# Letting GpSimd subtract the rounded weights in the SSD stage of a two-block network kernel

## The reference

```
u = rmsnorm(h); z, xbc, dt_raw, q, k, v, g_ssd, g_att = split_cols(u @ w_in)
xbc = silu(causal_dwconv(xbc, conv_w, conv_b));  xs, bm, cm = split_cols(xbc)
dt = softplus(dt_raw + dt_bias);  a = -exp(a_log)
for each chunk of 128 tokens (the first has 16), for each of 4 groups of 8 heads:
    L = exp(cs_l - cs_s) below the diagonal, cs = cumsum(dt * a)
    y = ((C B^T) * L) (x dt)  +  exp(cs) * C state
    state = exp(cs_last) * state + B^T (decay * x dt)
y = y + d_skip * x;  y = group_rmsnorm(y * silu(z)) ;  y_ssd = y @ w_ssd_branch
```

## Time and profile before

| what | value |
|---|---|
| median of 3 runs | 2701.64 us (2695.93 to 2713.91) |
| the profiled execution | 2691.95 us |
| its span, first to last instruction | 2690.0 us |
| TensorE busy | 2522.0 us (94%) |
| VectorE busy | 1632.3 us (61%) |
| ScalarE busy | 899.1 us (33%) |
| GpSimd busy | 62.2 us (2%) |
| mean granted TensorE clock | 0.965 of full |
| SSD stage's loop | about 1386 to 1862 us of the span |

### The profile page before, as it was taken

The page is one execution under the profiler, slowest core; times in us unless marked ns, Lnnn a source line. Parts: engine busy times, 40 slices in busy tenths (PEclk is TensorE's granted clock), DMA queues, the critical chain, the costliest instruction groups (busy, mean ns, idle before and its releaser), DMA issues.

```text
span 2690.0 us, 40344 instructions
## 1 busy us (share of the span) xinstructions
PE 2522.0 (94%) x15581; PEld 2210.7 (82%) x15581; DVE 1632.3 (61%) x2776; ACT 899.1 (33%) x1341; POOL 62.2 (2%) x55
## 2 busy tenths in 40 slices
PE   6999999998988999999989899889998999999997
PEld 4887888876887987888888788879777789999997
DVE  6556444456387845444587687877554555884684
ACT  3122222234354532222336634652232233222222
POOL 0000000000021000000000000001000000000000
PEclk9999999999988999999999999989998999999998
DMA  4235222334441012222225223412111112223222
GB/s 139 94 102 124 94 94 94 135 118 121 137 114 41 24 63 83 94 94 94 94 80 126 80 71 108 112 58 90 45 54 50 56 63 95 78 88 117 93 94 95
DMA packets 89708, 242.46 MB, mean 90 GB/s; under 512 B 24870, under 2 KB 56102, under 8 KB 65574
## 3 DMA queue, kind: packets, MB, share of 16 engines
q1 hardware_dynamic: 29056, 198.26, 20.7%
q10 hardware_dynamic: 58744, 36.42, 6.2%
q0 software_dynamic: 1760, 5.77, 1.0%
HBM read 230.50 MB, written 11.14 MB: 90 GB/s over the span
## 4 chain that ended last, share of the span: by engine, by line
PE 48%; DVE 8%; issue 3%; ACT 2%; ACTq 0%; DVEq 0%
PE ps L1151 26%; PE ps L927 13%; PE ps L1239 3%; DVE wlo L1389 1%; PE ps L1327 1%; PE ps L1294 1%; ACT L L776 1%; PE ps L1329 1%; PE ps L1330 1%; PE ps L1310 1%; PE ps L1313 0%; PE ps L1293 0%; ACT whi L506 0%; PE ps L1202 0%; PE ps L1204 0%
## 5 line engine op out<-in xcount | busy, mean ns | idle before, releaser
L506 ACT ACTIVATE whi<-raw 128x2048 fp32r<-128x2048 f32 x187 | 357.6, 1912 | 754.3 <-PE ps L927 501.5
L1151 PE MATMUL ps<-parts,whi 128*128 128x264 f32 x2752 | 488.6, 295 | 5.3 <-issue 4.7
L1389 DVE TENSOR_TENSOR wlo<-raw,whi 128x2048 fp32r<-128x2048 f32 x187 | 427.4, 2286 | 66.6 <-ACT whi L506 65.8
L927 PE MATMUL ps<-parts,whi 128*128 128x512 f32 x1360 | 435.0, 401 | 14.7 <-DVE wlo L1389 9.9
L1151 PEld LDWEIGHTS ps<-parts,whi 128*128 128x128 f32 x2752 | 396.2, 193 | 19.4 <-issue 16.7
L927 PEld LDWEIGHTS ps<-parts,whi 128*128 128x128 f32 x1360 | 259.0, 191 | 80.0 <-DVE wlo L1389 9.3
L927 PE MATMUL ps<-parts,wlo 128*128 128x512 f32 x680 | 271.8, 400 | 0.0
L1151 PE MATMUL ps<-parts,wlo 128*128 128x264 f32 x1200 | 247.4, 288 | 0.0
L927 PE MATMUL ps<-Mhi,whi 128*128 128x512 f32 x512 | 203.2, 397 | 5.1 <-DVE Mlo L1480 5.1
L927 PE MATMUL ps<-Mhi,wlo 128*128 128x512 f32 x512 | 203.0, 396 | 0.0
L927 PE MATMUL ps<-Mlo,whi 128*128 128x512 f32 x512 | 203.0, 396 | 0.0
(11 more groups left out here) (355 smaller groups left out, 4050.4 us busy)
## 6 DMA issues: line engine op xcount, KB each, us to landing
raw<-in_stream SPq DMA_DIRECT2D x187, 1024.0 KB, 4.8
csb<-sums_d ACTq DMA_DIRECT2D x16, 512.0 KB, 5.6
bands<-scratch ACTq DMA_DIRECT2D x6, 1024.0 KB
near<-bands ACTq DMA_DIRECT2D x20, 256.0 KB, 2.6
csf<-sums_d ACTq DMA_DIRECT2D x32, 128.0 KB, 6.0
Qst<-parts POOLq DMA_DIRECT2D x14, 256.0 KB, 6.3
tabs<-bands ACTq DMA_DIRECT2D x8, 418.0 KB, 3.0
X<-in_x SPq DMA_DIRECT2D x4, 512.0 KB, 14.8
```

The lines of the kernel that those rows point to most:

```text
L506: nc.scalar.activation(whi[:, s, :], raw[:, s, :], ACT.Copy).then_inc(hi_done, 1)
L927: mm = nc.tensor.matmul(out, w[:, s, at], x(k), start=k + j == 0, stop=k == k_tiles - 1 and j == 2)
L1151: mm = nc.tensor.matmul(ps[:, 2 * par + h, 0:HALF], w[:, s, at], x[:, k, h * HALF:(h + 1) * HALF], start=k + j == 0, stop=k == k_tiles - 1 ...
L1389: nc.vector.tensor_tensor(wlo[:, s, :], raw[:, s, :], whi[:, s, :].bitcast(F32), ALU.subtract).then_inc(lo_done, 1)
```

## The change

In the SSD stage, VectorE's 28 calls of `split_low` are taken out. GpSimd does the subtraction in four instructions of 512 columns a unit, two at a step: parts 0 and 1 at the even steps from 2 on, parts 2 and 3 at the odd ones, each time behind the Hd multiply of that step if there is one. The last two parts of the last unit come after the step loop. `lo_done` rises with the fourth part. VectorE gets one wait of its own for `lo_done` before its next subtract, in "kv2".

```diff
+            def split_low(c, turn, part):
+
+                u = U0["half"] + c + 2
+                s, at = u % 2, slice(part * SEQ, (part + 1) * SEQ)
+                if part == 0:
+                    pool.wait_ge(hi_done, turn + (u + 1))
+                    pool.wait_ge(lo_done, turn + u)
+                low = nc.gpsimd.tensor_tensor(wlo[:, s, at], raw[:, s, at], whi[:, s, at].bitcast(F32), ALU.subtract)
+                if part == 3:
+                    low.then_inc(lo_done, 1)
...
                         nc.gpsimd.tensor_tensor(Hd[:, :].rearrange("p (h d) -> p h d", h=SSD_HPG), Hs[:, :].rearrange("p (h d) -> p h d", h=SSD_HPG),
                                                 decay, ALU.mult).then_inc(hd_ready, 1)
+                    if r > 1:
+                        for part in (0, 1) if r % 2 == 0 else (2, 3):
+                            split_low(r // 2 - 1, i * 14, part)
+                for part in (2, 3):
+                    split_low(13, i * 14, part)
...
-                    if r and r % 2 == 0:
-                        split_low("half", r // 2 - 1, i * 14)
...
-                    if r % 2:
-                        split_low("half", r // 2, i * 14)
...
+            dve.wait_ge(lo_done, U0["kv2"] + 2)
             split_low("kv2", 0)
```

## The result

The kernel after takes 2711.01 us (median of 20 runs, 2705.62 to 2723.67); the kernel before took 2700.99 us beside it (20 runs, 2686.43 to 2713.91). The ratio is 1.0051, with an interval of 1.0034 to 1.0067: half a per cent slower, well inside 1%. The forecast was 2696, the likeliest case a small gain. The time lies inside the range of 8 in 10 (2683 to 2713), but on the other side of no change, nearer to rival one (2717).

The account below looks back on a forecast made before the run. TensorE, busy 94%, sets the time; in the SSD stage it waits for VectorE. Terms sum to -2.1 us a pass, twice -4.2, with (h) -1.8: -6.0, median 2696 us; range of 8 in 10: 2683 to 2713.

Parts of the forecast that it names:

- rival one: SSD stage: GpSimd/VectorE lock and late parts compound, clock falls at steps 10 and 16; slower, 2717 us; chance 0.2.
- (a): Steps 9 to 11: removed subtracts save at most 2.8 us a pass; with collisions, -0.8 taken.
- (d): Step 15: decay multiply comes sooner, at most 2.2 of a 4.40 us wait; -1.5 us a pass taken.
- (f): Step 17: subtract ahead of the multiply goes, 2.2 of 2.94 us plus slow stretch; -3.0 us a pass.
- (g): Step 20: subtracts ahead of YNlo and the last Gv add go; -3.3 us a pass after 0.7 collision.
- (h): Once, at the stage's end: subtract ahead of the output scale goes; -1.8 us of a 2.20 us wait.
- (b): Step 8: last parts, queued behind Hd, finish after TensorE's half tile would start; +0.7 us a pass.
- (c): Step 10: last parts, queued behind Hd, finish after TensorE's half tile would start; +2.8 us a pass.
- (e): Step 16: last parts behind Hd come late for TensorE; 2.4 us, with some collision +3.0 a pass.
- the shared resource: GpSimd and VectorE hold each other up; each part can stop a VectorE instruction wanting two SBUF inputs up to 1.25 us.
- point of decision: Sign deciding for rival one: a part holds VectorE for more than 1 us in most scan steps.
- I cost it at nothing: SP's stream load waits for the same semaphore; with at least 10 us spare before ScalarE rounds, its delay costs nothing.

Follow-up runs that it names:

- small_dve: Kernel before, with VectorE's subtract in the stage cut to 4 columns (that work left out): 2666.65 us, ratio 0.9870.
- small_pool: Kernel after, with GpSimd's parts cut to 4 columns at the same queue places (that work left out): 2678.56 us, ratio 0.9912.
- early: Kernel after, with all four parts of a unit at the even step, none at odd steps: 2706.7 us, ratio 1.0021.
- extra_pool: Kernel before, VectorE's subtracts kept, plus 112 GpSimd subtracts of 128x512 on their own tiles that nobody waits for: 2726.74 us, ratio 1.0083.
- whole: Kernel after, with one GpSimd instruction of 2048 columns per unit at the even step instead of four parts: 2739.19 us, ratio 1.0146.
- c12_dve: Kernel after, with one unit of each pass (c = 12, awaited by the pass's last load) subtracted by VectorE again: 2701.19 us, ratio 1.0003.
- branch_only: Kernel before, with only units 10 to 13 (branch sums) moved to GpSimd, four parts at the even step: 2705.02 us, ratio 1.0017.
- second_only: Kernel before, with only units 6 to 9 (second group's scans and norm) moved to GpSimd, four parts at the even step: 2684.18 us, ratio 0.9950.

## Why the prediction was wrong

The mechanism was seen and its size was not. The kernels make a chain from before to after, in us of the whole stage; beside each link stands what the sum had for it:

| link | measured | in the sum |
|---|---|---|
| before to small_dve: VectorE's subtract goes | -30.8 | -26.2: (a) 2.8, (d) 2.2, (f) 3.0 and (g) 4.0 twice, (h) 2.2 |
| small_dve to small_pool: GpSimd's instructions in their places, tiny | +5.6 | nothing |
| small_pool to early: full length, TensorE no longer waiting for them | +29.0, of which 2.2 at the pass boundary | +8.4 (hold), nothing (boundary) |
| early to after: the last parts a step later, behind Hd | +11.0 | +11.8: (b) 0.7, (c) 2.8 and (e) 2.4 twice |
| before to after | +14.8 | -6.0 |

(small_pool has a slow stretch of its own at the boundary; against before the boundary costs 4.2 us in early.) The hold in the sum is 2.0 us in (a), 0.7 in (d), 0.6 in (e) and 0.7 in (g), twice, and 0.4 in (h). Each link is a difference of two single profiled executions. The ratios, over all runs, check them: as us of 2701 they give the stage's difference from before to within 5 us for eleven of the twelve kernels (after 13.8 against 14.8, small_dve -35.1 against -30.8, extra_pool 22.4 against 23.2, whole 39.4 against 44.1); only c12_dve lies further off, 0.8 against 8.2. So the links of 29.0 and 30.8 are large against this, and those of 5.6 and 11.0 are not by much. extra_pool gives the hold again, by another way, as +23.2; and the ratios give the cost of the parts' length with the last link (29.0 and 11.0): 1.0051 less 0.9912 is 1.4%, 37 us against 40.

The step that failed is **the shared resource**. It took the hold at 4.0 us a pass, 8.4 in all, reasoned from single collisions, and weighed a part only where it fell ahead of one of TensorE's waits. The hold measured 23 us in extra_pool and 27 to 29 in the chain; the lateness and the gain came near their terms. The runs show the hold as a loss of VectorE's time everywhere: 48 us of busy time for 112 parts in extra_pool, 0.43 us a part, and 52 of 64 us in after. The rule that I had cited (the Trainium skill, "SBUF — State Buffer", section "SBUF: two separate sides": an exclusive lock, the loser blocked for the whole instruction) agrees with the 5.0 us of whole; I had read it as a reason for a rival and not as the price. Rival one (2717) had the mechanism and came within 6 us, in part by luck: it let the clock fall at step 16, where it didn't fall, took steps 9 to 11 for a loss, where after has a gain, and had nothing for the pass boundary. Its own point of decision, more than 1 us in most scan steps, is about what was measured: two parts a step at 0.43 us are 0.9.

Term by term:
- **(a)** -0.8 predicted. Step 9 waits 0.38 instead of 1.13 us, step 10 0.48 for Hs as before, step 11 nothing. That is a gain of 2.0 in the first pass, but it rests on the stop of 3.64 us in between: without it, in early, the same steps lose.
- **(b)** 0.7 predicted; 0.65 and 0.67 in the two passes.
- **(c)** 2.8 predicted; 3.64 in both passes, and the clock fell behind it, which the forecast left to rival one: four matmuls 1.25 us instead of 0.73.
- **(d)** -1.5 predicted; 4.40 became 3.51, and in the second pass 2.91 became 3.49 with the slow stretch (sixteen matmuls in 1.97 us). The gating multiply ahead of it took 1.82 us instead of 0.71, held by a part: 1.1 us, where the sum had allowed 0.7. The gain is 0.9 us in the first pass, with the slow stretch gone, and in the second a loss of 0.6.
- **(e)** 3.0 predicted; 2.33 and 1.87.
- **(f)** right: no wait at step 17 in either pass.
- **(g)** -3.3 predicted. The wait for YNlo fell from 3.73 to 2.05, and the one of 1.82 for the Gv add is gone. But seven YNlo in a row took 6.87 us where they had taken 4.83, so the evacuation behind them is late: TensorE waits 1.95 us for it (L1843), in the second pass 3.48. And 1.52 us for the last YNlo stand where the Gv wait was. In all, the waits for VectorE here fell from 5.99 to 5.52 us in the first pass and from 7.13 to 6.08 in the second: a gain of about 0.5 and 1 us, where 3.3 had been summed.
- **(h)** 2.20 became 1.30: a gain of 0.9, not 1.8.
- **"I cost it at nothing"**, of SP's load: no wait for the load of the unit of step 10 was seen. For the last one of a pass it was not nothing (4.5 us); the cover that I named (ten us until ScalarE rounds) guards the data, and I had not looked at what else runs while the load does.
- The gain of taking the subtract away is 30.8 us against the 26.2 that the sum started from, and 31.2 with all of the slow stretches that (d) and (f) named. In the stage the matmuls' busy time moved by 12.4 us for 18.4 us of idle time removed.

That TensorE's pause is longer because of the load is supported by its going with it over all thirteen profiles: 3.10, 3.15, 2.88 and 2.64 us with a DMA share of 0.89 to 0.96 in the 2.3 us ahead of it (after, branch_only, early, whole), and 1.34 to 1.93 us with one of 0.02 to 0.30 in the other nine; and c12_dve, which issues that load earlier, brought it down as expected. What in the pause the load delays is not shown: theory C's fetch of the loop's instructions stays a guess. Nor is it settled why the clock fell after some waits and not after others: 1.97 us for the sixteen matmuls after 3.49 us, but 1.09 after 3.51. And of the 11 us between early and after, 3.1 are idle time and 7.9 the clock, in one profile each; the intervals of their ratios overlap (1.0042 and 1.0034).

## What to carry to other kernels

An instruction moved to GpSimd beside a busy VectorE is not priced by the time it takes on GpSimd; price it by what it takes back from VectorE, here 52 of 64 us, and cut it small. Move such work only into stretches in which VectorE has idle time and TensorE waits for it (second_only, -0.5%): its busy time hardly falls there either (1.1 us), but the work no longer stands ahead of what TensorE waits for. And ask of each moved step what stands ahead of it in an in-order queue and where the transfer that it releases will land. Where TensorE's clock falls behind its waits, price a wait by more than its length, but expect no fixed rate: here the same matmuls gave back 12.4 us for 18.4 us of waits removed, and took 10.1 for 4.7 added in after, but 6.1 for 17.1 in extra_pool.

## What I had not expected of the hardware

- The hold lasts for a whole instruction and shows in the *duration* of VectorE's, not in its idle time: a 0.77 us convolution step took up to 1.72 us beside parts of 1.3 us, and up to 5.01 us beside 4.6 us. The median stays 769 ns, so only the mean and the longest tell it. Evacuations, which read PSUM, stayed at 0.71 us.
- GpSimd's subtract took 1.26 us for 512 columns at the shortest and 4.51 for 2048, 3.6 times as long.
- TensorE's pause at a loop's restart was 1.36 us with quiet queues and 3.10 us when 1 MB was being loaded; over the thirteen kernels 1.34 to 1.93 and 2.64 to 3.15.
